# Three result tiles' gates in the last scan step, and added instead of subtracted weight remainders, in a two-layer hybrid decoder step

## The reference, cut to what matters

```python
proj = x @ w_in                       # z, xBC, dt, q, k, v, and two gates of 1024 columns each
gate_ssm  = sigmoid(proj[..., OFF_G:OFF_G + 1024])
gate_attn = sigmoid(proj[..., OFF_G + 1024:])
y_ssm, conv_new, h_new = ssd_mixer(z, xbc, dt_raw, ...)   # 8 groups: conv, chunked scan, gate, norm
o_attn, kv_rows = dilated_mixture_attention(q, k, v, ...)
merged = gate_ssm * (y_ssm @ w_ssm_br) + gate_attn * (o_attn @ w_attn_br)
x = layer_norm(ALPHA * x + merged @ w_o)
x = layer_norm(ALPHA * x + square(relu(x @ w_up)) @ w_down)
```

## Time and profile before

| what | us |
|---|---|
| median of the runs | 2704.57 |
| the profiled execution's own time | 2710.73 |
| its span, first to last instruction | 2709.0 |
| PE busy | 2563.6 (95%) |
| DVE busy | 1176.1 (43%) |
| ACT busy | 1148.9 (42%) |
| POOL busy | 833.7 (31%) |
| last scan step, layer 0, from its first transpose to the first branch product | 41.83 |
| from there to the first product with `wab` | 20.15 |

### The profile page before, as it was taken

One profiled execution on the slowest core, in us unless ns is written; L12 is line 12 of the kernel. 1 busy time (PEld: TensorE's weight loads), 2 busy tenths in 40 slices (PEclk: granted clock), 3 DMA queues, 4 the chain that ended last, 5 costly groups with the idle time before them and its releaser, 6 DMA issues.

```text
span 2709.0 us, 52013 instructions
## 1 busy us (share of the span) xinstructions
PE 2563.6 (95%) x21394; PEld 2432.2 (90%) x21408; DVE 1176.1 (43%) x1907; ACT 1148.9 (42%) x1686; POOL 833.7 (31%) x563
## 2 busy tenths in 40 slices
PE   7989999999899999999999799999989999999997
PEld 7967898988799999999989579899979998999997
DVE  3443677777411541021253536777773117210213
ACT  3252676775322253132242527677652223422322
POOL 4312111111333353443353031111114343434331
PEclk9989999999899999999999899999999999999998
DMA  4225467666222222222222255776742222222221
GB/s 141 84 114 195 124 191 197 182 182 171 68 91 81 88 69 87 85 85 89 83 89 85 98 212 151 183 186 188 198 124 84 88 85 71 86 86 86 88 91 65
DMA packets 78859, 321.64 MB, mean 119 GB/s; under 512 B 9840, under 2 KB 9904, under 8 KB 72288
## 3 DMA queue, kind: packets, MB, share of 16 engines
q1 hardware_dynamic: 51264, 182.74, 20.4%
q0 software_dynamic: 27424, 136.47, 18.4%
HBM read 290.09 MB, written 29.07 MB: 118 GB/s over the span
## 4 chain that ended last, share of the span: by engine, by line
PE 76%; DVE 8%; ACT 5%; DMA 4%; issue 3%; DVEq 1%; POOL 1%; ACTq 1%; SPq 0%; POOLq 0%
PE acc L426 21%; PE acc L427 20%; PE acc L429 20%; DMA out_stout<-region 2%; DVE region L1477 1%; PE acc L473 1%; DVE region L1595 1%; DVE region L1589 1%; PE px L758 1%; PE acc L858 1%; DMA wring_parts<-in_wst 1%; PE px L770 1%; PE px L698 1%; PE px L620 1%; PE px L458 1%
## 5 line engine op out<-in xcount | busy, mean ns | idle before, releaser
L426 PE MATMUL acc<-xhi,whi 128*128 128x272 f32 x3552 | 987.4, 296 | 9.2 <-DMA wring_parts<-in_wst 5.9
L427 PE MATMUL acc<-xlo,whi 128*128 128x272 f32 x3552 | 958.2, 289 | 0.0
L1735 POOL TENSOR_TENSOR wring_parts<-wring,whi 128x1024 fp32r<-128x1024 f32 x258 | 628.6, 2439 | 930.1 <-ACT whi L908 915.2
L429 PE MATMUL acc<-xhi,wring_parts 128*128 128x272 f32 x3552 | 736.4, 288 | 0.0
L908 ACT ACTIVATE whi<-wring 128x1024 fp32r<-128x1024 f32 x340 | 358.7, 1055 | 815.6 <-DMA wring<-in_wst 705.8
L426 PEld LDWEIGHTS acc<-xhi,whi 128*128 128x128 f32 x3552 | 669.1, 188 | 30.0 <-issue 25.6
L427 PEld LDWEIGHTS acc<-xlo,whi 128*128 128x128 f32 x3552 | 669.0, 188 | 2.8
L429 PEld LDWEIGHTS acc<-xhi,wring_parts 128*128 128x128 f32 x3552 | 555.5, 188 | 0.0
L426 PE MATMUL acc<-region_parts,whi 128*128 128x272 f32 x1792 | 487.8, 291 | 15.4 <-DVE big_parts L1658 8.0
L427 PE MATMUL acc<-big_parts,whi 128*128 128x272 f32 x1536 | 417.6, 290 | 0.0
L429 PE MATMUL acc<-region_parts,wring_parts 128*128 128x272 f32 x1792 | 373.8, 290 | 0.0
(11 more groups left out here) (236 smaller groups left out, 2798.3 us busy)
## 6 DMA issues: line engine op xcount, KB each, us to landing
wring<-in_wst SPq DMA_DIRECT2D x340, 512.0 KB, 3.3
wring_parts<-in_wst POOLq DMA_DIRECT2D x82, 512.0 KB, 6.7
region<-scratch_ac POOLq DMA_DIRECT2D x16, 1088.0 KB, 8.4
region<-in_st POOLq DMA_DIRECT2D x16, 1024.0 KB, 6.3
out_stout<-region POOLq DMA_DIRECT2D x16, 1024.0 KB, 7.5
big<-in_kc POOLq DMA_DIRECT2D x16, 768.0 KB, 6.6
big<-in_vc POOLq DMA_DIRECT2D x16, 768.0 KB, 7.5
out_kv<-region POOLq DMA_DIRECT2D x2, 3264.0 KB, 10.2
```

The costliest lines, as they stand in the source:

```text
L426: nc.tensor.matmul(o, w_hi_, hi, start=first, stop=False)
L427: nc.tensor.matmul(o, w_hi_, lo, start=False, stop=False)
L429: mm = nc.tensor.matmul(out[:, 512 * h:512 * h + HT], w_lo_, parts(h)[0], start=False, stop=last)
L1735: pool.tensor_tensor(wlo[:, slot, :], whole[:, slot, :], whi[:, slot, :].bitcast(F32), ALU.subtract)\
```

## The change

- The last scan step gets six units: the gates of result tiles 0, 1 and 2 (`EARLY_GATES`). The units' order in `U_MRG` is changed to match: pairs 0 to 2 are gates 0 to 2, then branch 0, gate 3, branch 1, gate 4, and so on to branch 4, gate 7, then branches 5, 6 and 7 in a row (`gate_pair`, `branch_pair`). The host packs the weights in that order.
- ACT's part of the last step takes the gates in between: 0's and 1's first before the root, three behind or around it, and the sixth behind the eighth of the sixteen roundings of y. The gates lie in five buffers, two of them where the convolution's buffers were, two where the B and C rows were; ACT waits for `post_ready` and `st_st` for these.
- The rounding of y waits for `ns_done` (PE's product for the new states) where it waited for `ns_add` (DVE's addition of it).
- `ADDED` goes up to unit 97: units 68 to 97 get a second pass on ACT and an adding transfer, and POOL subtracts none of them.
- The loops over result tiles are written out, on PE, ACT, DVE and POOL.

The diff, cut to its core:

```diff
-ADDED = range(U_GRP + 6 + AHEAD, U_MRG + 2)
+EARLY_GATES = 3
+ADDED = range(U_GRP + 6 + AHEAD, U_WO)
...
+def gate_pair(m):
+    return m if m < EARLY_GATES else 2 * m - EARLY_GATES + 1
+def branch_pair(m):
+    return EARLY_GATES + min(2 * m, m + KT - EARLY_GATES)
...
+        gates_of = [gates, *early_gates, gates, *late_gates, gates, late_gates[0]]
...
@@ PE, group @@
-                        elif k < 2:
-                            gemm(L, T_MRG, 0, k, [unit_of(L, U_MRG + k)], x_parts, between)
                         else:
-                            for _ in range(4):
-                                between()
+                            gemm(L, T_MRG, gate_pair(k // 2), k % 2, [unit_of(L, U_MRG + k)], x_parts, between)
...
@@ PE, behind the groups @@
-                with pe.Fori(0, KT - 1) as m:
+                for m in range(KT):
                     branches(m)
-                    for k in range(2):
-                        gemm(L, T_MRG, 2 * m + 2, k, [unit(L, U_MRG + 4 + k, m)], x_parts)
-                branches(KT - 1)
+                    if m + EARLY_GATES < KT:
+                        pair = gate_pair(m + EARLY_GATES)
+                        for k in range(2):
+                            gemm(L, T_MRG, pair, k, [unit_of(L, U_MRG + 2 * pair + k)], x_parts)
...
@@ ACT, last step @@
-                        for k in range(2, NC + 1):
-                            decay(k)
+                        decay(2)
+                        gate(0, 0)
+                        decay(3)
+                        decay(4)
+                        gate(0, 1)
                         copy_y()
+                        act.wait_ge(post_ready, 32 * L + 32)
+                        gate(1, 0)
                         square()
                         root()
-                        gate(0, 0)
-                        gate(0, 1)
+                        gate(1, 1)
+                        gate(2, 0)
...
                 act.wait_ge(yssm_ready, 16 * L + 16)
-                act.wait_ge(ns_add, 8 * L + 8)
+                act.wait_ge(ns_done, 8 * L + 8)
                 act.wait_ge(h_st, 128 * L + 128)
                 for k in range(D_IN // P):
+                    if k == KT:
+                        gate(2, 1)
                     nc.scalar.activation(yhi[:, k, :], yssm[:, k, :], ACT.Copy).then_inc(yh_ready, 1)
...
@@ POOL, last step and merging @@
-                    elif not projects:
-                        low(L, last)
...
+                    low_added(L, u + AHEAD)
+                    low_added(L, u + 1 + AHEAD)
...
-                low(L, U_MRG + AHEAD)
-                low(L, U_MRG + 1 + AHEAD)
+                low_added(L, U_MRG + 2 * EARLY_GATES - 1 + AHEAD)
                 hold(pool, yssm_ready, 16 * L + 16)
...
```

More of the change, by code:

```diff
@@ L262, in build @@
         assert reg.at <= 4 * T
+        late_gates = [reg.take(2, T) for _ in range(2)]
+        assert reg.at <= after_stores
+        reg.restart(after_qkv)
+        early_gates = [reg.take(2, T) for _ in range(2)]
+        assert reg.at <= after_qkv + 4 * RAWW
         reg.restart(after_group)
         gates = reg.take(2, T)
+        gates_of = [gates, *early_gates, gates, *late_gates, gates, late_gates[0]]
         xde2.append(reg.take(256))
@@ L1034, in gate @@
                 def gate(m, k):
-                    high(L, U_MRG + k + AHEAD, m)
-                    unit_done(unit(L, U_MRG + k, m))
+                    u = U_MRG + 2 * gate_pair(m) + k
+                    high(L, u + AHEAD)
+                    unit_done(unit(L, u))
                     b = (T_MRG + k) % 2
-                    nc.scalar.activation(halves(gates[:, k, :]), two(acc[b]), ACT.Tanh, scale=0.5)
+                    nc.scalar.activation(halves(gates_of[m][:, k, :]), two(acc[b]), ACT.Tanh, scale=0.5)
                     act.drain().then_inc(acc_free[b], 1)
@@ L1659, in _ @@
                       .then_inc(y_split, 1)
-                with dve.Fori(0, KT) as m:
+                for m in range(KT):
+                    gates = gates_of[m]
                     dve.drain()
@@ L1665, in _ @@
                     dve.drain()
-                    unit_done(unit(L, U_MRG + 3, m))
+                    unit_done(unit(L, U_MRG + 2 * branch_pair(m) + 1))
                     b = (T_MRG + 2) % 2
@@ L1675, in _ @@
                     dve.drain()
-                    hi, lo = (v[:, bass.ds(m, 1), :].rearrange("p a n -> p (a n)") for v in (mhi, mlo))
+                    hi, lo = (v[:, m, :] for v in (mhi, mlo))
                     nc.vector.tensor_copy(hi, prod[:, 0, :])
@@ L1855, in group @@
                         pad_states(g)
-                    last = U_GRP + 6 * gs + 5 + AHEAD
-                    if last in ADDED:
-                        low_added(L, last)
-                    elif not projects:
-                        low(L, last)
-                    if projects:
-                        low_added(L, u + AHEAD)
-                        low_added(L, u + 1 + AHEAD)
+                    if not projects:
+                        u = U_MRG
+                    if u - 1 + AHEAD in ADDED:
+                        low_added(L, u - 1 + AHEAD)
+                    low_added(L, u + AHEAD)
+                    low_added(L, u + 1 + AHEAD)
                     hold(pool, h_ready, 4 * s + 4)
@@ L1892, in load_wab @@
                     pool.dma_start(wab, row(A["wab"], L * KT + m, "o p k n -> (o p) k n")).then_inc(wab_ld, 16)
-                    for k in range(2, 4):
-                        low(L, U_MRG + k + AHEAD, m)
-                with pool.Fori(0, KT - 1) as m:
+                    for u in (U_MRG + 2 * branch_pair(m) + AHEAD, U_MRG + 2 * branch_pair(m) + 1 + AHEAD):
+                        if u in ADDED:
+                            low_added(L, u)
+                        else:
+                            low(L, u)
+                for m in range(KT):
                     load_wab(m)
-                    for k in range(4, 6):
-                        low(L, U_MRG + k + AHEAD, m)
-                load_wab(KT - 1)
+                    if m + EARLY_GATES < KT:
+                        for k in range(2):
+                            low_added(L, U_MRG + 2 * gate_pair(m + EARLY_GATES) + k + AHEAD)
                 for k in range(KT):
@@ L1977 @@
         u += [x for g in range(GROUPS) for x in (bb[g], cc[g], xs[2 * g], xs[2 * g + 1], z[2 * g], z[2 * g + 1])]
-        u += [x for m in range(KT) for x in (gs[m], ga[m], br[m, 0], br[m, 1])]
+        merged = [None] * (2 * KT)
+        for m in range(KT):
+            merged[gate_pair(m)] = (gs[m], ga[m])
+            merged[branch_pair(m)] = (br[m, 0], br[m, 1])
+        u += [x for pair in merged for x in pair]
         u += list(tiles(i["w_o"][l])[:, 0])
```

33 lines of the change are left out of this document (18 added, 15 removed).

## The result

The changed kernel takes 2660.86 us, the median of four runs (2657.96 to 2671.82); the kernel before took 2705.28 us in the runs beside them. The ratio is 0.9838 (95% interval 0.9811 to 0.9865). Forecast was 2661, 2655 to 2673. Medians and ratios in this document leave out two executions that ran slow as a whole, at a clock of 0.74 and 0.56: one of the kernel before (3173.31 us) and one of the adding transfers alone (4187.84 us).

What follows compares the result with a forecast made beforehand. TensorE, busy 95% of the span, bounds the kernel; only its idle or low-clock time can be won. 46.7 - 2.9 - 0.3 = 43.5 us off the 2704.6 median gives 2661 us, range 2655 to 2673.

Steps and rivals of the forecast that it cites:

- The unit and the stage: Loop unit 6.02 us at full clock; last step's start to end of first branch's second unit 63.22 us.
- part 1: Last scan step gets six units, not two; two gate pairs leave each layer's loop: 46.7 us saved in both layers.
- y in time: Start of first branch: its rounded input y arrives without a wait, slack 2 us or more, cost nothing.
- The rounds: Loop over result tiles: adding transfers cost nothing, slack 6 us, at worst 3; some 167 GB/s in 25.92 us.
- Rival 2: Loop's adding transfers land too late: gain eaten at chain 21.4 us (no change 0.03), or slower, 2731 (0.05).
- The 2.9 us at the third unit of the last step: Adding transfer issued behind the states' load lands late: PE waits 0.8 and 2.1 us; bounds 0 and 4.
- The 0.3 us at the first `wab` and gate: First attention weights and gate unit queue behind the awaited new-states store on GpSimd: 0.3 us in all; bounds 0 and 4.
- Descriptor writing beside DVE: DVE's sixteen subtractions could hold up GpSimd's transfer issues at the branches' start; left out of the sum.
- Rival 1: GpSimd held up at branches' start, gate unit and attention weights late: 4.4 us per layer, 2670; chance 0.16 with Rival 3.
- Rival 3: ACT late at gates in last step, PE idles: 4 us per layer, 2669, or 12, 2686; chance 0.16 with Rival 1.

Runs made afterwards that it cites:

- the adding transfers alone: Changed kernel with two units in the last scan step and the old unit order, all remainders still added by transfers: 2707.69 us, ratio 1.0006 to the kernel before.
- the early gates alone: Changed kernel with remainders of units 68 to 97 subtracted by GpSimd as before: 2665.74 us, ratio 0.9854 to the kernel before.
- Both drain experiments: Changed kernel with the convolution copy and drain ahead of the state load: 2654.88 us; or with the drain removed, the copy signalling itself: 2654.91 us.

## Why the prediction was right, point by point

- **The unit and the stage: right, in mechanism and in number.** 63.22 us were forecast for the stage, 63.06 measured in both layers. The gain of part 1 is 48.16 - 1.18 = 47.0, forecast 46.7. This step carries the result, and the early gates alone show it apart: 0.9854 of 0.9838.
- **y in time.** ACT began the rounding at 700.05, right behind the new-states product, DVE its first eight pieces at 702.20, and PE has no wait for either at the start of the branch. The ninth piece, which the gate in the middle delays, was ready at 710.4 and PE wanted it at 712.0: 1.6 us to spare where I had 2 or more. Putting the wait for the addition back changed nothing.
- **The rounds.** 25.92 us as forecast, at 167 GB/s as forecast. The slack of 6 us, at worst 3, stands in the trace: 5.3 to 6.3 us for half of the transfers, 3.2 at the least. A hold that leaves one unit costs 50 us. Rival 2 was thus a real danger with a real margin, and the change stays on the near side of it: no transfer in the rounds was waited for. What I had left out of its price is that `wab` stands behind the transfers on GpSimd's queue.
- **The 2.9 us at the third unit of the last step: wrong, it was 0 in both layers.** I took the 7.75 us of the earlier trace rows for something that follows a load of states. The row shows only that GpSimd's queue stood; what stood in it, a drain behind the convolution's copy, is in the program between load and transfer, and the last step has none. Both drain experiments show it. The 13.9 us that spoke for rival 2 hold the same drain. The term's lower bound, 0, was the right value, and the sum would then have been 2658.
- **The 0.3 us at the first `wab` and gate: 0.** `wab` was issued at 710.82, 55.9 us after the step's start, where I had put it at 57.5; PE took it 63.06 us after the start without a wait. Rival 1's late start didn't come.
- **Descriptor writing beside DVE.** The longest issue of an adding transfer was 1.214 us in the whole run; the one at 710.23, beside DVE's second eight subtractions, took 0.95. The Trainium skill ("DMA: Bandwidth & Descriptors", section "SWDGE vs HWDGE vs iDMA") says that the descriptor rings are SBUF state which DVE locks GpSimd out of in its 2-port performance mode. No run here shows such a hold; none shows either whether these subtractions run in that mode, so the rule isn't refuted.
- **Rival 3, ACT late in the last step.** The only wait left there is 0.38 us for the squares, as in a projecting step. Of the six gates ACT takes three ahead of the root, two behind it and the last among the roundings.
- **What made the time come out at 2661 rather than 2658.** That the number is met to the microsecond is luck in part: 3.2 us of waits that I had priced didn't come, and about as much was lost elsewhere. Probably it was the waits in the projecting steps, which I took as the same before and after. In the two profiled executions they cost 7.1 and 14.0 us. Whether the change makes them larger isn't shown. By the same count they cost 8.5 us with the early gates alone, and 4.2 to 17.8 in the five other profiled executions with all remainders added and the drain in its place, so that one execution decides nothing. With the drain moved away the kernel before gained 6.7 us, the changed one 6 by the ratios, so on the median they are about equal.

## What to carry to other kernels

Independent matrix units, put where one engine's product waits for another's vector work, give back the idle time, the low clock behind it and the queueing that the late start causes; count all three, and take them from the stretch as it will be. When a queue stands still in a trace, look up every instruction that the program has at that place before naming the cause, also those that the profile doesn't count as busy: a drain behind an issued transfer can be the whole wait. An adding transfer is free only while its chain fits; ask also what stands behind it on its queue.

## What the runs showed of the hardware that I had not expected

- A drain on GpSimd behind a 1 MB load that it had issued held it until that load had landed: 6.0 to 8.0 us in twelve steps, with the next issue 1.0 to 1.1 us after the landing each time. Without the drain the next issue followed the copy at once.
- A wait of PE of 4.34 us cost 6.1 us, since the clock stood at 0.55 and then 0.76 for the 4.7 us behind it.
- A multiplication of 0.43 us on DVE took 3.81 us beside two of GpSimd's subtractions in a row and ended 0.3 us after them. Of the sixteen subtractions on DVE two took 2.96 and 2.91 us beside GpSimd's, the others some 0.72.
